# One adaptive block and its successor on one core: the modulation and first norm by quarters of the features instead of halves, with the state space model eight units later

## What is computed

```
mod = silu(c) @ w_ada + b_ada          # 2048 -> 6 * 2048: sh1, sc1, g1, sh2, sc2, g2
h   = rms_norm(x, norm_mix_g) * (1 + sc1) + sh1
u, q, k, v, ga, gb = split(h @ w_in)   # widths 1024, 1024, 1024, 1024, 2048, 2048
y_ssm = s5_branch(u, ...)              # a scan over the tokens, 64 groups, then gelu and a gated w_glu
y_att = attention(q, k, v)             # 8 heads of 128, causal, with a bias by distance
x = x + g1 * ((sigmoid(ga) * (y_ssm @ w_proj_ssm) + sigmoid(gb) * (y_att @ w_proj_attn)) @ w_out)
```

## Time and profile before

| what | value |
|---|---|
| median of three runs | 3000.74 us (2994.73 to 3001.56) |
| profiled execution, its own time | 3000.71 us |
| span in its profile | 2999.4 us |
| TensorE matmul busy | 2931.9 us, 98% |
| VectorE busy | 2023.6 us, 67% |
| ScalarE busy | 1379.4 us, 46% |
| mean DMA rate | 211 GB/s, with 350 and 329 GB/s in the first two of 40 slices |

### The profile page before, as it was taken

How to read it: one execution, slowest core, us unless ns; L and a number is a source line. 1 busy time by engine, 2 the same in 40 slices (tenths; PEclk the granted TensorE clock), 3 DMA queues, 4 the chain that set the end, 5 groups by cost and what they waited for, 6 DMA issues and landing times.

```text
span 2999.4 us, 42350 instructions
## 1 busy us (share of the span) xinstructions
PE 2931.9 (98%) x17149; PEld 2513.0 (84%) x17149; DVE 2023.6 (67%) x2359; ACT 1379.4 (46%) x1686; POOL 239.4 (8%) x256
## 2 busy tenths in 40 slices
PE   6999999999999999999999999999999999999998
PEld 3778899788888888888989987778898888888886
DVE  5489878997767655556887776674557545555555
ACT  3343344444444444345565655554445444444443
POOL 6835410000000000000000000000000000000000
PEclk9999999999999999999999999999999999999999
DMA  9967688896777766665556565456555666666664
GB/s 350 329 213 210 209 295 297 302 319 203 236 257 257 235 187 193 194 186 172 174 171 196 174 192 155 155 161 195 186 176 175 190 189 188 192 190 192 192 191 149
DMA packets 303520, 631.67 MB, mean 211 GB/s; under 512 B 21872, under 2 KB 26384, under 8 KB 302752
## 3 DMA queue, kind: packets, MB, share of 16 engines
q1 hardware_dynamic: 298496, 618.74, 64.9%
q10 hardware_dynamic: 2800, 5.33, 0.5%
q0 software_dynamic: 2032, 4.90, 0.5%
HBM read 624.68 MB, written 4.21 MB: 210 GB/s over the span
## 4 chain that ended last, share of the span: by engine, by line
PE 86%; DVE 7%; DMA 3%; issue 2%; ACT 1%; ACTq 0%; DVEq 0%
PE PS L1026 16%; PE PS L1042 15%; PE PS L1044 15%; PE PS L1043 15%; PE PS L1030 8%; PE PS L1013 5%; PE PS L1015 5%; PE PS L1014 5%; DVE wlo L1991 2%; DMA raw<-in_w_ada 1%; DVE aacc L1980 1%; ACT whi L2519 1%; PE PS L691 1%; DMA raw<-in_w_in 1%; PE PS L824 1%
## 5 line engine op out<-in xcount | busy, mean ns | idle before, releaser
L1991 DVE TENSOR_TENSOR wlo<-raw,whi 128x1024 fp32r<-128x1024 f32 x857 | 1070.4, 1254 | 729.6 <-ACT whi L2519 729.1
L2519 ACT ACTIVATE whi<-raw 128x1024 fp32r<-128x1024 f32 x857 | 904.5, 1059 | 1077.2 <-PE PS L1044 570.1
L1042 PE MATMUL PS<-whi,R 128*128 128x512 f32 x2144 | 847.2, 395 | 7.3 <-DVE R L1496 5.4
L1043 PE MATMUL PS<-whi,R 128*128 128x512 f32 x2144 | 836.0, 390 | 0.0
L1044 PE MATMUL PS<-wlo,R 128*128 128x512 f32 x2144 | 835.9, 390 | 0.0
L1026 PE MATMUL PS<-R,whi 128*128 128x512 f32 x2048 | 516.5, 394 | 10.8 <-DVE R L1903 5.4
L1042 PEld LDWEIGHTS PS<-whi,R 128*128 128x128 f32 x2144 | 403.0, 188 | 102.1 <-issue 7.6
L1044 PEld LDWEIGHTS PS<-wlo,R 128*128 128x128 f32 x2144 | 402.9, 188 | 85.6
L1043 PEld LDWEIGHTS PS<-whi,R 128*128 128x128 f32 x2144 | 403.2, 188 | 81.5 <-issue 1.0
L1013 PE MATMUL PS<-R,whi 128*128 128x256 f32 x1536 | 439.8, 286 | 7.5 <-DVE wlo L1991 6.0
L1026 PEld LDWEIGHTS PS<-R,whi 128*128 128x128 f32 x2048 | 371.3, 190 | 78.4 <-issue 11.5
(11 more groups left out here) (424 smaller groups left out, 1728.8 us busy)
## 6 DMA issues: line engine op xcount, KB each, us to landing
raw<-in_w_in SPq DMA_DIRECT2D x275, 512.0 KB, 4.3
raw<-in_w_ff SPq DMA_DIRECT2D x175, 512.0 KB, 4.4
raw<-in_w_ada SPq DMA_DIRECT2D x136, 512.0 KB, 5.2
raw<-in_w_mlp_up SPq DMA_DIRECT2D x128, 512.0 KB, 3.8
raw<-in_w_mlp_down SPq DMA_DIRECT2D x128, 512.0 KB, 4.4
F<-in_w_ff SPq DMA_DIRECT2D x81, 512.0 KB, 4.4
F<-in_w_ada SPq DMA_DIRECT2D x56, 512.0 KB, 6.3
raw<-in_w_out SPq DMA_DIRECT2D x53, 512.0 KB, 4.1
```

The source lines that it names most:

```text
L1042: pe.matmul(o, hi, whi[:, s, w], start=first, stop=False)
L1043: pe.matmul(o, lo, whi[:, s, w], start=False, stop=False)
L1991: v.tensor_tensor(wlo[:, i % SPN, :], words(j), whi[:, i % SPN, :].bitcast(F32), ALU.subtract).then_inc(lo_done, 1)
L2519: a.activation(whi[:, i % SPN, :], words(j), ACT.Copy).then_inc(hi_done, 1)
```

## The change

- The rows come by quarters of the features: a unit is one contraction tile by 512 columns of sh1 and the same 512 of sc1, 16 units a quarter. A close and a norm of four tiles follow each quarter. The closes use one bank, the norm tiles two, and the factor `rstd1` is copied from PSUM to SBUF by ScalarE.
- The five `part` panels become fifteen of two units each, one set of five for each of the first three quarters of h; sets two and three are added by VectorE to what stands in SBUF (`part_more`, ten new adds of 128 x 1024). The panels u and ga 0 to 2 run over the last quarter, two units each. All panels together have the same units and matmuls as before.
- 27 weight units instead of 17 are taken between the rows, from the 19th row on instead of the 34th.
- The turning of x moves from tick -58 to -61; the first factor moves ahead, the angles and parameters from ticks -54 and -51 to -47 and -46, the four matrices to ticks -38, -24, -11 and 28 (from -47, -46, -45 and -27).
- `SSM0` goes from 24 to 32. The first value panel runs ahead of the first query and key panels, heads begin 5, 8, 11 and 14 ticks after the first key panel and 2, 5, 8 and 11 after the second. The first value copy waits for six gelu steps, gate panels gb 1 and 3 are read out one tick later behind a wait for GpSimd, and the two extra slots for staging open at unit 105 instead of 97.

```diff
-NTAKEN = 17
+QUARTER = 16
+NTAKEN = 27
 NEARLY = NTAKEN + 3
-TAKEN = {33: 0} | {36 + n * 27 // (NTAKEN - 1): n + 1 for n in range(NTAKEN - 1)}
-EARLY = {31: (0,)} | {a - 3: (n,) for a, n in TAKEN.items() if n} | {61 + n: (NTAKEN + n,) for n in range(3)}
+TAKEN = {18 + n * 16 // 10: n for n in range(NTAKEN)}
+EARLY = {a - 3: (n,) for a, n in TAKEN.items()} | {61 + n: (NTAKEN + n,) for n in range(3)}
-SSM0 = 24
+SSM0 = 32
...
-    for i in range(5):
-        panel("part", i, w_in, 0, 8, i * 512 if i < 2 else 4096 + (i - 2) * 512, h, by_h, a_once.at("part%d" % i), i > 1)
+    for q in range(3):
+        for i, c0 in enumerate(halved):
+            panel("part", 5 * q + i, w_in, 4 * q, 4, c0, h_from[q], by_quarter(q),
+                  (part_added, 5 * q + i - 4) if q else a_once.at("part%d" % i), i > 1)
     for i in range(2):
-        panel("u", i, w_in, 8, 8, i * 512, h_b, by_h_b, (evac_v["u"], i + 1))
+        panel("u", i, w_in, 12, 4, halved[i], h_from[3], by_quarter(3), (evac_v["u"], i + 1))
...
-        for name, c0 in (("q", 1024), ("k", 2048), ("v", 3072)):
+        for name, c0 in (("q", 1024), ("k", 2048), ("v", 3072)) if i else (("v", 3072), ("q", 1024), ("k", 2048)):
...
+    def row_src(q, kt):
+        return wada[kt * P:(kt + 1) * P, 0:2 * D].rearrange("p (g d) -> p g d", g=2)[:, :, 512 * q:512 * q + 512]
...
-        units.append(("row", a, 1, ada_src(a % 2, a // 32, a % 32 // 2)))
+        units.append(("row", a, 2, row_src(a // QUARTER, a % QUARTER)))
...
-            (at_unit[97], at_unit[440], pair(RAWN, V, V + 1024), (y_done, 16)))
+            (at_unit[105], at_unit[440], pair(RAWN, V, V + 1024), (y_done, 16)))
...
-    MATRIX = (-NADA + 17, -NADA + 18, -NADA + 19, -NADA + 37)
-    MATRIX_TURN = (-NADA + 23, -NADA + 26, -NADA + 30, -NADA + 40)
-    ROW_CLOSE, NORM1 = [-33, len(TAKEN)], [-32, len(TAKEN) + 1]
+    MATRIX = (-NADA + 26, -NADA + 40, -NADA + 53, len(TAKEN) + 1)
+    MATRIX_TURN = (-NADA + 31, -NADA + 45, -NADA + 58, len(TAKEN) + 3)
+    ROW_COPY = [-NADA + 15 + QUARTER * q for q in range(4)]
+    ROW_CLOSE = [-NADA + 15, -NADA + 32, -NADA + 48, len(TAKEN)]
...
-    HEAD_TICK = [end_of["v", i] + t for i in range(2) for t in (2, 3, 4, 11)]
+    HEAD_TICK = [end_of["k", 0] + t for t in (5, 8, 11, 14)] + [end_of["k", 1] + t for t in (2, 5, 8, 11)]
...
+        def part_more(x):
+            i, q = x.i % 5, x.i // 5
+            v.wait_ge(*passed("part", x.i))
+            v.wait_ge(*(a_once.at("part%d" % i) if q == 1 else (part_added, i + 1)))
+            v.tensor_tensor(half_sum(i), banks(x), half_sum(i), ALU.add).then_inc(part_added, 1)
+            yield
...
+        def gate_b_later(x):
+
+            yield
+            a.wait_ge(z_used, 8)
+            tanh_half(x, fv(GB + 1024 * x.i, 1024), evac_a["gb"])
```

More of the change, by code:

```diff
@@ L304, in program @@
     nb = lambda v, k=4: v.unsqueeze(1).broadcast_to([P, k, T])
-    h, h_b, yg, ys, ya, mg, h2, hid = (Operand(R, *b) for b in ((0, 1), (1,), (2,), (0,), (3,), (1, 2), (0, 3), (1, 2)))
+    h_from = [Operand(R, 0, 1, first=4 * q) for q in range(4)]
+    h, yg, ys, ya, mg, h2, hid = (Operand(R, *b) for b in ((0, 1), (2,), (0,), (3,), (1, 2), (0, 3), (1, 2)))
     HU, H, xc, YA, MG, H2, HID = (Operand(R, *b) for b in ((0, 3), (1, 2), (0, 3), (0, 3), (1, 2), (0, 3), (1, 2)))
@@ L686, in row_matmuls @@
                 pe.wait_ge(*v_once.at("cact"))
-            if n == 32:
-                wait_bank(row_bank[1])
+            elif kt == 0:
+                wait_bank(row_bank[q])
+                free[row_bank[q]] = row_copied, q + 1
             for part in range(4):
                 o = 32 * part
-                t = pe.matmul(PS[o:o + 1, row_bank[q], g * T:g * T + T], cact[:, kt:kt + 1], words(j)[:, part * T:part * T + T],
-                              start=(n % 32 == 0), stop=(kt == 15), skip_group_check=True)
+                t = pe.matmul(PS[o:o + 1, row_bank[q], 0:T], cact[:, kt:kt + 1], words(j)[:, part * T:part * T + T],
+                              start=(kt == 0), stop=(kt == QUARTER - 1), skip_group_check=True)
             t.then_inc(row_done, 1)
         def row_close(q):
-            bank = row_close_bank[q]
             pe.wait_ge(row_copied, q + 1)
-            if q:
-                wait_bank(bank)
-            for g in range(2):
-                for c in range(2):
-                    o = 512 * q + T * g + P * c
-                    t = pe.matmul(PS[:, bank, 8 * g + 4 * c:8 * g + 4 * c + 4], aacc[:, o:o + P], ident[:, 0:P:32],
-                                  start=(g + c == 0), stop=True, skip_group_check=True)
+            wait_bank(row_close_bank)
+            for c in range(2):
+                o = T * q + P * c
+                t = pe.matmul(PS[:, row_close_bank, 4 * c:4 * c + 4], aacc[:, o:o + P], ident[:, 0:P:32],
+                              start=(c == 0), stop=True, skip_group_check=True)
             t.then_inc(row_turned, 1)
-            if q:
-                for bank in (4, 5, 6, 7):
-                    free[bank] = (h_ready, 16)
-            yield
+            free[5] = free[6] = h_ready, 4 * q + 4
         def acc_close(g, bank):
@@ L1070, in side @@
             if n in ROW_CLOSE:
-                new.append(row_close(ROW_CLOSE.index(n)))
+                row_close(ROW_CLOSE.index(n))
             if n == end_of["k", 0] + 2:
@@ L2039, in evacuation @@
             i = x.i
+            if x.name == "part":
+                return [part_more(x)] if i > 4 else []
             if x.name == "u" or x.name == "ga" and i < 3:
@@ L2098, in columns, with factor1, angles @@
             t.then_inc(a_once.sem, 1)
+        def factor1():
+            a.wait_ge(*p_once.at("stat1"))
+            a.copy(rstd1, PS[:, 4, T:2 * T]).then_inc(a_once.sem, 1)
+        def angles():
             a.wait_ge(*a_once.at("cols"))
@@ L2177, in norm1 @@
         def norm1(q):
-            for n in range(8):
-                k = 8 * q + n
+            for k in range(4 * q, 4 * q + 4):
                 a.wait_ge(n1_scaled, k + 1)
                 a.activation(h.hi(k), norm_tile(k), ACT.Identity, bias=mod[:, k:k + 1]).then_inc(n1_hi, 1)
-            yield
         def banks(x):
@@ L2512, in main @@
                 setup()
+            if n in ROW_COPY:
+                row_copy(ROW_COPY.index(n))
             for j in prepared(n):
@@ L2524, in side @@
                 new.append(x_copies())
+            if n == STD1:
+                deviation1()
             if n == COLUMNS:
                 columns()
-            if n == B_TURN + 1:
+            if n == B_TURN:
                 b_copy()
+            if n == FACTOR1:
+                factor1()
+            if n == ANGLES:
+                angles()
             if n == -NADA + 53:
@@ L2598, in evacuation @@
             i = x.i
+            if x.name == "part" and i > 4:
+                return []
             if x.name == "part":
```

134 lines of the change are left out of this document (67 added, 67 removed).

## The result

The changed kernel takes 3014.95 us (median of 4 runs, 3013.27 to 3019.2) where the kernel before takes 3000.73 beside it: a ratio of 1.0054 with a 95% interval of 1.0036 to 1.0071 (a ratio is worked out from all runs and not from the two medians, whose quotient is 1.0047). It is slower by about 14 us, outside the range and on the side that had a chance of 0.10. The profiled executions have spans of 3012.6 and 2999.4, so 13.2 of difference to explain, and with the 7.3 forecast as a gain 20.5.

A forecast was written before the change was run, and what follows sets the result against it. DMA was taken to bound the first 64.6 us, TensorE what follows. Gains and losses of +8.3 - 1.1 - 1.1 + 1.2 = 7.3 us took 3000.7 to 2993.4, stated as 2993, range 2983 to 3003.

The forecast's parts named there:

- the side that had a chance of 0.10: Whole kernel slower than before: DMA becomes the bound (3011 us, chance 0.08) or other stalls; chance 0.10 together.
- When the first unit can start: Before the first weight unit between the rows: it starts at about 42.2 us instead of 64.6.
- From there to 28 units: First weight unit to the 28th: 116.7 us, done at 158.9; 19.5 later for 27.8 of work, net 8.3 gained.
- Rival C: At the three later turns of quarters: each costs 2.8 us of waits, total 2999.7, no change; chance 0.14.
- Behind the rows: After the last row group: one matrix moved there costs 1.1 us, TensorE's waits 5.3 against 4.2 cost another 1.1.
- the state space model keeps its distance: Behind the rows: the model begins five ticks behind them instead of seven, its last step still four ticks ahead of its reader.
- The sum for the matrix: VectorE's queue behind unit 27: TensorE can turn the fourth matrix 10.9 to 12.3 us on, so stands 2.3 to 3.7.
- Is DMA slower than that?: Between the rows: at 1.45 us a unit the last row lands at 149.5, TensorE reaches it at 155.9 and sets the pace.
- rival E: GpSimd's tables are late: start 49.6, end 157, decisive only if contention adds 30 us; about 3001; chance 0.04.
- Heads and glu: At the moved heads and the stall behind glu: 1.2 us gained, bounds -2 and +7.9.
- Cover the same: Staging slots that open at unit 105: four units are left with four slots, so no change in cover.
- What would make it wrong: Test of the prediction: 28 units done outside 155 to 163, or a new stall behind 212.

## Why the prediction was wrong, by its own steps

- **When the first unit can start**: predicted 42.2, measured 44.59, as TensorE's rows show:

```profile
42.26 1.03 PE L710 MATMUL PS<-F,der 128*1 128x256 f32 x8 [2.09 <-DMA F<-in_w_ada]
...
44.59 0.58 PE L1025 MATMUL PS<-R,whi 128*128 128x256 f32 x1
```

  Three row groups stand ahead of the unit, and TensorE waits 2.1 us for one of them to land. The first tile of h is ready at 42.40 (VectorE's line 1348), as forecast. The step asked when h is ready, not when the groups queued ahead have landed. Off by 2.4.
- **From there to 28 units**: predicted 158.9, measured 163.4, 4.5 late: the 2.4 of the start, and the rest at the third turn. Rival C's wait appears at that one (2.2 us, with a granted clock of 0.73 and 0.50 in the 4 us from 128 on), at the other two later turns there is none of over 0.5. The net gain at this point was 3.8 (27.8 less 24.0), not 8.3. The size was off, the mechanism right. The last row group ended at 160.4, outside the 154 to 158 given.
- **Behind the rows**: this is the step that failed. "Together 5.3 against the 4.2 of today" stands against waits of 17.4. It counted VectorE's queue for durations, and the moved model by its distance to its reader ("the state space model keeps its distance"), but not the count that these parts share. 11.9 us are a wait that only a later event ends, because the gate panels had come ahead of the product table. The runs split the total: 5.5 us for the count, 7.2 more for the save of x (6.6 and 6.2 in the other order), which the prediction did not name as moved, although its tick is set by the number of units taken between the rows (21 before, 31 in the changed kernel). With both cured, the waits are 5.5 and the term as predicted would have been right. The time is then still 3002.2 and not 2993.4: the 28 units came 6.9 later than forecast, at 165.8, and from 228 to 600 TensorE stands 6.9 us against the 4.7 that the forecast implies (5.9 less 1.2), 2.2 more. The low clock behind waits was given no price. In the changed kernel it is 0.50 and 0.73 over the 4 us from 218 on, after TensorE had stood 11.9 us; six matmuls take 2.73 us there (218.19 to 220.92) and 1.36 at the full pace of the earlier trace rows, so 1.4 us are lost.
- **The sum for the matrix** in that step holds a slip: 5.1 + 1.8 + 3.5 to 4.9 is 10.4 to 11.8 and not 10.9 to 12.3, so the wait comes out as 1.8 to 3.2. Measured is 2.0 (line 762), inside that and just under the recorded 2.3 to 3.7.
- **Is DMA slower than that?** 1.51 us for a unit against 1.45, under the 1.53 named: right, by little. TensorE's waits for `w_ada` behind 60 us sum to 1.6, under the 6 named.
- **GpSimd's tables** (rival E): the last operation ends at 157.65, 157 was predicted; not late. That it is so near is partly luck: the tables begin at 51.58 and not at 49.6, and take 106.1 us and not 107.5. The adds in its argument on shared interfaces read PSUM and SBUF, so the rule named there does not cover them; one took 1.21 us beside GpSimd (at 207.54).

```profile
156.92 0.73 POOL L2761 TENSOR_TENSOR F<-F 128x252 f32<-128x252 f32 x1
```

- **Heads and glu**: +1.2 predicted, +2.8 alone in the kernel before; in the changed kernel the wait at `ps` is 2.5 (3 to 5 were named), and 2.7 us of waits for casts stand against it between 420 and 560. That is 0.3 gained from 228 to 600, 5.6 against 5.9. "Cover the same", of the slots at unit 105, put a term at nothing: between 420 and 534 TensorE never waits in the kernel before, and the changed kernel and its variants have waits of 0.5 to 3.8 us at unit 105 or 106. Why they appear is open.
- **What would make it wrong** named both signs: 28 units outside 155 to 163 and a stall that is not there now. Both came, the second from 206.3 to 218.2.

In the sum 4.5 ahead of 28 units and 17.4 less 5.3 behind it are 16.6 of the 20.5. The trace adds 1.4 for the low clock behind the long wait and 0.9 for the heads' term (1.2 forecast, 0.3 found). The rest, 1.6, stays open.

## What to carry to other kernels

When a part is moved, list every event that shares a counter with it and check in the trace that the order of the events is still that of the list: a count out of order gives no error message. It releases the waiters of the overtaken places one event late, and that of the late event too early, before its data is there. Then a semaphore of its own is right, or a proof that another wait covers the reader. When "n units earlier" is bought by a schedule that is keyed to a unit number, look at what else is keyed to it, a bulk transfer above all, and into which engine's full stretch it now falls. And a lead on the bounding engine is kept here only as far as the next engine's full stretch: ask which engine's queue ends last there, with the products, adds and casts summed over the whole stretch.

## What the runs showed of the hardware

VectorE's products with both inputs in SBUF took 2.30 and 2.31 us at 203 to 207.6, while GpSimd multiplied (its rows are busy from 202.13 to 208.80), and 1.21 us at 213.27 with GpSimd idle; the add at 207.54 with one input in PSUM took 1.21 beside GpSimd. The Trainium skill says in GPSIMD Engine Reference, Specifications, that GpSimd and VectorE share their memory interfaces, with contention when an instruction of VectorE has two inputs in SBUF. These rows agree, and here it is a factor of 1.9 on 4.6 us in the stretch that VectorE bounds. The factor is not the same everywhere: a cast at 201.97, with both inputs in SBUF, took 1.20 us although GpSimd's record begins at 202.13. GpSimd's rows of the changed kernel:

```profile
202.13 2.18 POOL L2795 TENSOR_TENSOR F<-F 128x512 f32<-128x512 f32 x1 [17.79 <-DVE F L1428]
...
208.12 0.68 POOL L2800 TENSOR_TENSOR F<-F 128x256 f32<-128x256 f32 x1
224.57 2.20 POOL L2795 TENSOR_TENSOR F<-F 128x512 f32<-128x512 f32 x1 [15.78 <-DVE F L1428]
```

Packets of 2 KB took a median of 84 ns and of 4 KB 159 ns in the changed kernel, so half the size costs 6% in time per byte. Runs of 4 KB for all row units moved the median by 2 us of 3000, which the intervals do not tell from none.
